# GpSimd's splits of the weights and of the heads' operands issued in two pieces

## The chip, the cores and the metric

The kernel runs on one core of one Trainium2 chip. The metric is the device time of one execution in microseconds, as the median of several executions. Only one core runs, so there is no traffic between cores.

## The reference

Two blocks follow each other on one sequence of 1024 tokens with 1024 features, in float32. The first has a mixer (attention with 8 heads in three dilated windows, beside a diagonal state-space branch) and a gated feed-forward part with a short convolution. The second has three gated branches and a final norm. Cut to what the change touches:

```python
def _hybrid_mixer(u, w_in, ...):
    proj = u @ w_in                       # q, k, v, us and two gates
    q, k, v, us, g_att, g_ssm = jnp.split(proj, ...)
    o_att = <windowed attention of q, k, v, 8 heads of 64>
    y_att = o_att @ w_proj_att
    y_ssm = _s5_branch(us, ...) @ w_proj_ssm
    merged = sigmoid(g_att + gb_att) * y_att + sigmoid(g_ssm + gb_ssm) * y_ssm
    return merged @ w_out
# h = x + gt1 * _hybrid_mixer(...);  h = h + gt2 * _conv_ffn(_modulate(h, ...))
# then the second block: p = h @ w_in_2, three branches, merged @ w_o, norm
```

## The kernel before

Every large product is made from two halves of each operand: a high part (the value rounded to the type `fp32r` that TensorE reads fast) and a low part (the value less its high part). A product is three matmuls: high by high, high by low and low by high. The activations' parts lie in `act_h` and `act_l`, the weights' in `w_h` and `w_l`. Weights come in units of 256 output columns: SyncE loads one unit into `raw`, GpSimd (POOL in the profile) makes `w_h` and `w_l` of it, and TensorE (PE) uses it. `w_h` and `w_l` have two buffers, so the split of unit n waits until PE has finished unit n-2, and PE's unit n waits for the split of unit n.

Units are numbered through the program: unit 0 is the state-space input, 1 to 6 are q, k and v (`N_QKV`), 7 to 14 the gates (`N_GATE`), 15 to 18 the projections (`N_PROJ`, six rows of 128 instead of eight), 19 to 22 the mixer's output (`N_OUT`), 23 and 24 the first two of the feed-forward part (`N_FFN`). After these, weights are split in another way (`unit_weights` and `block_lows`, 512 columns in one instruction), up to the last four units (`N_WO`).

`split` handles a unit in two parts. Each part is a TENSOR_SCALAR that writes `w_h` (multiply by 1.0, which rounds), a wait on its own semaphore, and a TENSOR_TENSOR that writes `w_l`. The first part raises `w_half`, the second `w_split`. A part of a unit with eight rows of 128 is 4 x 256 = 1024 columns, of a projection unit 3 x 256 = 768, and of a unit with four rows 512. PE waits for `w_split` in `split_done` before it loads the unit's first weights.

In attention GpSimd also runs `stage(h)` for each head: five dependent instructions over 1024 columns on `q2`, `k_ll` and `k_hh`. PE needs head h staged before that head's first scores. Meanwhile PE fills the gaps between score, transpose and value matmuls with the gate units' matmuls, and VectorE (DVE) works through the first block's modulation weights in `ada_chunks`: a chain of 128x256 instructions that read two operands in SBUF (`ada_part` and a chunk of `w_ada`). Behind them on DVE's queue stand the copies of transposed probabilities (`near_half`, L2864), which PE waits for in `values`.

The mixer's output units 19 and 20 are used for all tokens, but units 21 and 22 for half the tokens at a time. So PE comes to unit 22 after four half products of 24 matmuls, the first of which starts when unit 20 is done:

```python
for th in range(2):
    for u in range(4):
        if th == 0:
            split_done(N_OUT + 2 + u // 2)
            pe.wait_ge(s["out_read"], AHEAD + u + 1)
        ...
        product_half(slot(u), 1 - u // 2, u % 2, KD, act_h, act_l, th, after=after)
```

The orders of all engines are written out by hand; nothing is scheduled by a planner. `single(n)` is `split` with the wait for PE's unit n-2 (`units_before(n - 1)`). DVE's residual sums and sums of squares (L2992, L3002) run beside the output units.

Of the kernel before, what the change touches and what calls it, by code (L numbers as in the profile page):

```python
# [8 lines left out]
ALU = mybir.AluOpType  # L9
F32 = mybir.dt.float32  # L10
# [3 lines left out]
T = 1024  # L14
D = 1024
KD = D // P
HALF = 512
# [73 lines left out]
def splits_before(n):  # L91

    return n - blocks_before(n) - min(max(n - N_DB, 0), DB)
# [78 lines left out]
def build(nc, a, out):  # L172
    ctx = ExitStack()
    with ctx:
# [3 lines left out]
        def at(name, shape, offset, dt=F32):  # L178

            return nc.alloc_sbuf_tensor_at(name, shape, dt, offset=base + offset)  # L180
# [6 lines left out]
        w_h = at("w_h", [P, 2, KD, NB], 64 * kib, F32R)  # L187
        w_l = at("w_l", [P, 2, KD, NB], 80 * kib, F32R)
# [89 lines left out]
        q2 = at("q2", [P, 2, T], 96 * kib, F32R)  # L278
        k_hh = at("k_hh", [P, 2, T], 104 * kib, F32R)
# [109 lines left out]
        s = {n: ctx.enter_context(nc.semaphore(n)) for n in names}  # L389
# [52 lines left out]
        def raw_of(n):  # L442

            return raw[:, 0 if N_GATE + 1 < n < N_PROJ + 2 else n % 2]
# [586 lines left out]
        def _(pool):  # L1031
# [9 lines left out]
            def split(n, k, landed, before=None, kc=KD, landed_ssm=None):  # L1041

                src = raw_of(n)
                pool.wait_ge(w_in_[k], landed)
                if landed_ssm:
                    pool.wait_ge(ws_in[k], landed_ssm)
                if before is not None:
                    pool.wait_ge(s["gemm"], before)
                pool.sem_inc(s["passed"], 1)
                for half, done in enumerate((s["w_half"], s["w_split"])):  # L1050
                    c = slice(half * kc // 2, (half + 1) * kc // 2)
                    nc.gpsimd.tensor_scalar(w_h[:, k, c, :], src[:, c, :], 1.0, None, ALU.mult).then_inc(s["w_high"], 1)  # L1052
                    pool.wait_ge(s["w_high"], 2 * splits_before(n) + half + 1)
                    nc.gpsimd.tensor_tensor(w_l[:, k, c, :], src[:, c, :],  # L1054
                                            w_h[:, k, c, :].bitcast(F32), ALU.subtract).then_inc(done, 1)

            def split_first():

# [46 lines left out]
            def single(n, kc=KD, landed_ssm=None):  # L1105
                split(n, n % 2, 16 * (n // 2 + 1), units_before(n - 1) if n >= 2 else None, kc, landed_ssm)

            stage_step = Steps(pool, s["staged"])
            stage_step.base = PREP_STEPS

            def stage(h):

                e = h % 2
                own, other = slice(0, HD), slice(HD, P)
                pool.wait_ge(head_in[e], 4 * 16 * (h // 2 + 1))
                q, k = q2[:, e, :], k_ll[:, e, :]
                stage_step(nc.gpsimd.tensor_scalar(k_hh[:, e, :], q.bitcast(F32), 1.0, None, ALU.mult))
                stage_step(nc.gpsimd.tensor_tensor(q2[other, e, :], q2[other, e, :].bitcast(F32),
                                                   k_hh[other, e, :].bitcast(F32), ALU.subtract))
                stage_step(nc.gpsimd.tensor_scalar(q2[own, e, :], q2[own, e, :].bitcast(F32), 1.0, None, ALU.mult))  # L1120
                stage_step(nc.gpsimd.tensor_scalar(k_hh[:, e, :], k.bitcast(F32), 1.0, None, ALU.mult))
                stage_step(nc.gpsimd.tensor_tensor(k, k.bitcast(F32), k_hh[:, e, :].bitcast(F32), ALU.subtract))

            pool.wait_ge(s["consts_ready"], CONSTS)
            pool.wait_ge(s["g_row_in"], 16)
# [7 lines left out]
            for n in range(1, N_GATE - 1):  # L1133
                single(n)
            stage(0)
            single(N_GATE - 1)
            stage(1)
            single(N_GATE)
            single(N_GATE + 1)
            for h in range(2, HEADS):  # L1140
                stage(h)
                single(N_GATE + h)
# [33 lines left out]
            def single_behind(n, m, i, kc):  # L1176

                pool.wait_ge(s["prod_done"], NPRE * (i - 1) + (5 if m else 2))
                split(n, n % 2, 16 * (n // 2 + 1), None, kc)
# [2409 lines left out]
```

## Time and profile before

| | |
|---|---|
| median of 3 executions | 1994.09 us (1992.82 to 1998.42) |
| profiled execution, its own time | 1995.31 us |
| span in its profile | 1993.6 us |
| granted TensorE clock | 0.999 |
| PE busy | 1971.0 us, 99% |
| DVE busy | 1143.7 us, 57% |
| ACT busy | 668.1 us, 34% |
| POOL busy | 1319.6 us, 66%, 795 instructions |

The profiled execution's own time is 1.7 us above its span, and 1.2 us above the median. Engines work side by side, so the busy times don't add up. PE's share says that TensorE is nearly always at work; another engine counts only where PE waits for it. In the timelines a row gives start, duration, engine, line, operation, output and inputs and, in brackets, how long the engine was idle before and what ended that. PEld is PE's loading of weights, which runs one matmul ahead.

### The profile page before, as it was taken

How to read it: one execution, taken by the hardware profiler on the slowest of the kernel's cores; microseconds unless marked ns; L12 is line 12 of the kernel's file. 1: busy time of each engine (PE TensorE's matmuls, PEld its weight loads, DVE VectorE, ACT ScalarE, POOL GpSimd, SP SyncE). 2: the span in 40 equal slices, each digit the busy share in tenths (PEclk: the TensorE clock that was granted, in tenths of full speed). 3: DMA queues.
4: the chain of work that ended last, by engine and by line, in shares of the span. 5: the costliest groups of instructions: out<-in, count | busy, mean ns of one | idle time of the engine just before them, and what ended most of it. 6: DMA issues, size and time to landing. Idle time of an engine off the chain costs nothing. (4 is left out here: it accounts for less than half of the span.)

```text
span 1993.6 us, 26010 instructions
## 1 busy us (share of the span) xinstructions
PE 1971.0 (99%) x10105; PEld 1639.9 (82%) x10105; DVE 1143.7 (57%) x1363; ACT 668.1 (34%) x1115; POOL 1319.6 (66%) x795
## 2 busy tenths in 40 slices
PE   8999999999999999999999999999999999999998
PEld 6888888888888787888888898888788888888888
DVE  6962378767652676656575386722464554624554
ACT  5213233233421454444321145433434433211103
POOL 4647457655364459999746538877787888858650
PEclk9999999999999999999999999999999999999999
DMA  9645564563644213333664422333323323198332
GB/s 336 201 118 160 172 185 151 159 199 115 216 161 156 85 64 106 103 130 106 234 251 159 148 86 64 119 115 112 120 77 136 127 85 106 34 377 317 117 137 86
DMA packets 195979, 295.41 MB, mean 148 GB/s; under 512 B 15416, under 2 KB 147472, under 8 KB 195856
## 3 DMA queue, kind: packets, MB, share of 16 engines
q1 hardware_dynamic: 185488, 270.55, 40.4%
q10 hardware_dynamic: 10368, 23.19, 3.1%
q8 instruction: 81, 1.33, 0.3%
q14 instruction: 42, 0.34, 0.1%
HBM read 213.73 MB, written 79.97 MB: 147 GB/s over the span
## 5 line engine op out<-in xcount | busy, mean ns | idle before, releaser
L1668 PE MATMUL ps<-tb,w_h 128*128 128x512 f32 x1344 | 416.9, 391 | 2.5 <-DVE quads L3056 1.9
L1052 POOL TENSOR_SCALAR w_h<-raw 128x512 fp32r<-128x512 f32 (+2 forms) x100 | 225.5, 2255 | 282.8 <-issue 127.1
L1173 POOL TENSOR_TENSOR w_l<-raw,w_h 128x512 fp32r<-128x512 f32 x210 | 309.5, 1483 | 92.6 <-ACT w_h L2307 92.6
L1668 PEld LDWEIGHTS ps<-tb,w_h 128*128 128x128 f32 x1344 | 251.3, 188 | 59.2 <-issue 3.9
L1668 PE MATMUL ps<-tb,w_l 128*128 128x512 f32 x672 | 261.5, 389 | 0.0
L2307 ACT ACTIVATE w_h<-raw 128x512 fp32r<-128x512 f32 x210 | 130.8, 627 | 236.8 <-PE ps L1668 150.3
L1668 PE MATMUL ps<-act_h,w_h 128*128 128x512 f32 x504 | 196.3, 389 | 0.6 <-ACT quads L2336 0.5
L1054 POOL TENSOR_TENSOR w_l<-raw,w_h 128x512 fp32r<-128x512 f32 (+2 forms) x100 | 191.3, 1913 | 8.3
L1668 PE MATMUL ps<-act_l,w_h 128*128 128x512 f32 x504 | 196.1, 389 | 0.0
L1668 PE MATMUL ps<-act_h,w_l 128*128 128x512 f32 x504 | 196.1, 389 | 0.0
L1668 PEld LDWEIGHTS ps<-tb,w_l 128*128 128x128 f32 x672 | 126.1, 188 | 26.3
L1241 PE MATMUL ps<-act_h,w_h 128*128 128x512 f32 x352 | 139.1, 395 | 0.8 <-DVE act_l L2671 0.5
L1241 PE MATMUL ps<-act_l,w_h 128*128 128x512 f32 x352 | 137.1, 389 | 0.0
L1241 PE MATMUL ps<-act_h,w_l 128*128 128x512 f32 x352 | 137.1, 389 | 0.0
L1668 PEld LDWEIGHTS ps<-act_h,w_h 128*128 128x128 f32 x504 | 94.6, 188 | 21.2 <-ACT quads L2336 1.1
L1668 PEld LDWEIGHTS ps<-act_h,w_l 128*128 128x128 f32 x504 | 94.6, 188 | 19.6
L1668 PEld LDWEIGHTS ps<-act_l,w_h 128*128 128x128 f32 x504 | 94.6, 188 | 19.5
L1340 PE MATMUL ps<-act_h,w_h 128*128 128x512 f32 x256 | 102.0, 398 | 1.3
L1340 PE MATMUL ps<-act_h,w_l 128*128 128x512 f32 x256 | 100.2, 391 | 0.0
L1340 PE MATMUL ps<-act_l,w_h 128*128 128x512 f32 x256 | 100.2, 391 | 0.0
L3056 DVE TENSOR_TENSOR quads<-ps,quads 128x512 f32<-128x512 f32 x42 | 28.9, 688 | 118.4 <-ACT quads L2333 116.5
L1173 POOL TENSOR_TENSOR w_l<-sum,w_h 128x512 fp32r<-128x512 f32 x56 | 79.4, 1419 | 20.1 <-ACT w_h L2307 18.0
(455 smaller groups left out, 4581.2 us busy)
## 6 DMA issues: line engine op xcount, KB each, us to landing
raw<-in_w_in SPq DMA_DIRECT2D x44, 1024.0 KB, 5.3
raw<-in_w_up SPq DMA_DIRECT2D x16, 1024.0 KB, 5.2
f_scratch<-r SPq DMA_DIRECT2D x16, 1024.0 KB, 8.3
gates_scratch<-quads SPq DMA_DIRECT2D x24, 512.0 KB, 7.6
r<-gates_scratch SPq DMA_DIRECT2D x12, 1024.0 KB, 6.4
ada_lo<-in_w_ada SPq DMA_DIRECT2D x16, 512.0 KB, 4.1
ada_hi<-in_w_ada SPq DMA_DIRECT2D x16, 512.0 KB, 4.4
gates_scratch<-gate_st ACTq DMA_DIRECT2D x32, 256.0 KB, 3.0
```

The source lines that it names most:

```text
L1052: nc.gpsimd.tensor_scalar(w_h[:, k, c, :], src[:, c, :], 1.0, None, ALU.mult).then_inc(s["w_high"], 1)
L1054: nc.gpsimd.tensor_tensor(w_l[:, k, c, :], src[:, c, :], w_h[:, k, c, :].bitcast(F32), ALU.subtract).then_inc(done, 1)
L1173: nc.gpsimd.tensor_tensor(w7_l[:, SLOTS[o]], x, w7_h[:, SLOTS[o]].bitcast(F32), ALU.subtract)\
L1241: last = nc.tensor.matmul(dst[:, tok], w[:, k, kw + c, P * cg:P * cg + P], x[:, c, tok], start=(c == 0 and p == 0), stop=(c == kc - 1 and ...
L1340: last = nc.tensor.matmul(gate_bank(g), w[:, n % 2, c, P * (j % 2):P * (j % 2) + P], x[:, c, tok], start=(c == 0 and p == 0), stop=(c == K ...
L1668: last = nc.tensor.matmul(bank_of(n, bank), w[:, SLOTS[o], c, :], x(c), start=(first and c == 0 and p == 0), stop=(c == KD // 2 - 1 and p ...
L2307: A.activation(w7_h[:, SLOTS[o]], src, ACT.Copy).then_inc(s["w7_high"], 1)
L3056: v.tensor_tensor(quad(n, 1), bank_of(n, "b"), quad(n, 0), ALU.add).then_inc(s["q_done"], 1)
```

## The change

Each of `split`'s two instructions for a part is issued as pieces of at most 512 columns, and each of `stage`'s five over 1024 columns as two over 512. Semaphores are raised only by the last piece, so every wait stands where it stood. A part of 1024 columns becomes two pieces of 512, one of 768 becomes 512 and 256, and one of 512 stays whole. `split_first`, `split_half`, `unit_weights` and `block_lows` are not touched. The other engines' instructions are the same.

```diff
@@ -1049,10 +1049,14 @@
                 pool.sem_inc(s["passed"], 1)
                 for half, done in enumerate((s["w_half"], s["w_split"])):
                     c = slice(half * kc // 2, (half + 1) * kc // 2)
-                    nc.gpsimd.tensor_scalar(w_h[:, k, c, :], src[:, c, :], 1.0, None, ALU.mult).then_inc(s["w_high"], 1)
+                    pairs = [slice(i, min(i + 2, c.stop)) for i in range(c.start, c.stop, 2)]
+                    for i in pairs:
+                        last = nc.gpsimd.tensor_scalar(w_h[:, k, i, :], src[:, i, :], 1.0, None, ALU.mult)
+                    last.then_inc(s["w_high"], 1)
                     pool.wait_ge(s["w_high"], 2 * splits_before(n) + half + 1)
-                    nc.gpsimd.tensor_tensor(w_l[:, k, c, :], src[:, c, :],
-                                            w_h[:, k, c, :].bitcast(F32), ALU.subtract).then_inc(done, 1)
+                    for i in pairs:
+                        last = nc.gpsimd.tensor_tensor(w_l[:, k, i, :], src[:, i, :], w_h[:, k, i, :].bitcast(F32), ALU.subtract)
+                    last.then_inc(done, 1)
 
             def split_first():
 
@@ -1112,14 +1116,25 @@
 
                 e = h % 2
                 own, other = slice(0, HD), slice(HD, P)
+                halves = (slice(0, HALF), slice(HALF, T))
                 pool.wait_ge(head_in[e], 4 * 16 * (h // 2 + 1))
                 q, k = q2[:, e, :], k_ll[:, e, :]
-                stage_step(nc.gpsimd.tensor_scalar(k_hh[:, e, :], q.bitcast(F32), 1.0, None, ALU.mult))
-                stage_step(nc.gpsimd.tensor_tensor(q2[other, e, :], q2[other, e, :].bitcast(F32),
-                                                   k_hh[other, e, :].bitcast(F32), ALU.subtract))
...
-                stage_step(nc.gpsimd.tensor_tensor(k, k.bitcast(F32), k_hh[:, e, :].bitcast(F32), ALU.subtract))
+                for tok in halves:
+                    last = nc.gpsimd.tensor_scalar(k_hh[:, e, tok], q[:, tok].bitcast(F32), 1.0, None, ALU.mult)
+                stage_step(last)
+                for tok in halves:
+                    last = nc.gpsimd.tensor_tensor(q2[other, e, tok], q2[other, e, tok].bitcast(F32),
+                                                   k_hh[other, e, tok].bitcast(F32), ALU.subtract)
+                stage_step(last)
...
+                for tok in halves:
+                    last = nc.gpsimd.tensor_tensor(k[:, tok], k[:, tok].bitcast(F32), k_hh[:, e, tok].bitcast(F32), ALU.subtract)
+                stage_step(last)
```

On GpSimd, at the split of unit 22 and the start of the split of unit 23, these instructions stood before (the brackets name the semaphores that an instruction waits for; `gemm` counts PE's finished products, `w_in` the landed loads):

```order
L1052 TENSOR_SCALAR w_h<-raw 128x1024 [waits w_in0,gemm]
L1054 TENSOR_TENSOR w_l<-raw,w_h 128x1024 [waits w_high]
L1052 TENSOR_SCALAR w_h<-raw 128x1024
L1054 TENSOR_TENSOR w_l<-raw,w_h 128x1024 [waits w_high]
L1052 TENSOR_SCALAR w_h<-raw 128x1024 [waits w_in1,gemm]
```

and these stand there now:

```order
L1054 TENSOR_SCALAR w_h<-raw 128x512 [waits w_in0,gemm]
L1054 TENSOR_SCALAR w_h<-raw 128x512
L1058 TENSOR_TENSOR w_l<-raw,w_h 128x512 [waits w_high]
L1058 TENSOR_TENSOR w_l<-raw,w_h 128x512
L1054 TENSOR_SCALAR w_h<-raw 128x512 x2
L1058 TENSOR_TENSOR w_l<-raw,w_h 128x512 [waits w_high]
L1058 TENSOR_TENSOR w_l<-raw,w_h 128x512
L1054 TENSOR_SCALAR w_h<-raw 128x512 [waits w_in1,gemm]
```

Each part's one instruction has become two. The second piece waits for nothing, and the wait on `w_high` stands ahead of the first subtracting piece as it stood ahead of the whole one.

On GpSimd, at the staging of a head in attention and the split of a gate unit behind it, these stood before:

```order
L1117 TENSOR_SCALAR k_hh<-q_128 128x1024
L1118 TENSOR_TENSOR q_128<-q_128,k_hh 64x1024
L1120 TENSOR_SCALAR q_128<-q_128 64x1024
L1121 TENSOR_SCALAR k_hh<-k_ll 128x1024
L1122 TENSOR_TENSOR k_ll<-k_ll,k_hh 128x1024
L1052 TENSOR_SCALAR w_h<-raw 128x1024
L1054 TENSOR_TENSOR w_l<-raw,w_h 128x1024
L1052 TENSOR_SCALAR w_h<-raw 128x1024
L1054 TENSOR_TENSOR w_l<-raw,w_h 128x1024
```

and these stand there now:

```order
L1123 TENSOR_SCALAR k_hh<-q_128 128x512 x2
L1126 TENSOR_TENSOR q_128<-q_128,k_hh 64x512 x2
L1130 TENSOR_SCALAR q_128<-q_128 64x512 x2
L1133 TENSOR_SCALAR k_hh<-k_ll 128x512 x2
L1136 TENSOR_TENSOR k_ll<-k_ll,k_hh 128x512 x2
L1054 TENSOR_SCALAR w_h<-raw 128x512 x2
L1058 TENSOR_TENSOR w_l<-raw,w_h 128x512 x2
L1054 TENSOR_SCALAR w_h<-raw 128x512 x2
L1058 TENSOR_TENSOR w_l<-raw,w_h 128x512 x2
```

The order is the same, each row is now two instructions of half the columns, and a head's ten pieces and the gate unit's eight run one after the other.

## Rows read from the trace of the kernel before

**Rows 1.** Busy us and instructions of each engine, clock, DMA: two stretches.
```profile
220.00:550.00 330.00, 325.37 (x2026) 272.48 (x2025) 229.90 (x384) 113.04 (x237) 180.90 (x71) 1.00 0.53 163
550.00:680.00 130.00, 130.00 (x579) 107.07 (x579) 61.36 (x63) 32.63 (x41) 72.16 (x28) 1.00 0.40 145
```

**Rows 2.** Groups of POOL instructions by shape: busy us, mean ns, idle before.
```profile
L1052 POOL TENSOR_SCALAR w_h<-raw 128x1024 fp32r<-128x1024 f32 x44 | 129.4, 2941 | 145.4 <-issue 75.9 <-DMA raw<-in_w_o 21.5 <-DMA raw<-in_w_in 16.5
L1054 POOL TENSOR_TENSOR w_l<-raw,w_h 128x1024 fp32r<-128x1024 f32 x44 | 109.1, 2480 | 3.7
```

**Rows 3.** Timeline of POOL: 512-column instructions, undisturbed.
```profile
682.96 1.29 POOL L1164 TENSOR_TENSOR sum_f<-sum_f,raw 128x512 f32<-128x512 f32 x1
684.20 1.30 POOL L1165 TENSOR_TENSOR raw<-raw 128x512 f32<-128x512 f32 x1
...
1769.56 1.50 POOL L1052 TENSOR_SCALAR w_h<-raw 128x512 fp32r<-128x512 f32 x1 [10.60 <-PE ps L1949]
1771.14 1.29 POOL L1054 TENSOR_TENSOR w_l<-raw,w_h 128x512 fp32r<-128x512 f32 x1
```

**Rows 4.** Timeline of POOL at the split of unit 22.
```profile
625.65 2.78 POOL L1052 TENSOR_SCALAR w_h<-raw 128x1024 fp32r<-128x1024 f32 x1 [9.50 <-issue]
628.52 2.40 POOL L1054 TENSOR_TENSOR w_l<-raw,w_h 128x1024 fp32r<-128x1024 f32 x1
630.89 2.77 POOL L1052 TENSOR_SCALAR w_h<-raw 128x1024 fp32r<-128x1024 f32 x1
633.74 2.40 POOL L1054 TENSOR_TENSOR w_l<-raw,w_h 128x1024 fp32r<-128x1024 f32 x1
```

**Rows 5.** Timeline of PE's weight loads: the first of unit 22.
```profile
636.19 0.19 PEld L1241 LDWEIGHTS ps<-act_h,w_h 128*128 128x128 f32 x1 [0.27 <-POOL w_l L1054]
```

**Rows 6.** Timeline of DVE in the same stretch: the sums of squares.
```profile
626.77 1.22 DVE L3002 TENSOR_TENSOR acc<-acc,sq 128x1024 f32<-128x1024 f32 x1
...
631.68 1.32 DVE L3002 TENSOR_TENSOR acc<-acc,sq 128x1024 f32<-128x1024 f32 x1
```

**Rows 7.** The split of unit 23: POOL's last instruction, PE's first load.
```profile
668.39 2.41 POOL L1054 TENSOR_TENSOR w_l<-raw,w_h 128x1024 fp32r<-128x1024 f32 x1
...
670.85 0.19 PEld L1241 LDWEIGHTS ps<-act_h,w_h 128*128 128x128 f32 x1 [0.29 <-POOL w_l L1054]
```

**Rows 8.** The split of unit 7: POOL's last instruction, PE's first load.
```profile
216.58 2.38 POOL L1054 TENSOR_TENSOR w_l<-raw,w_h 128x1024 fp32r<-128x1024 f32 x1
...
219.06 0.19 PEld L1340 LDWEIGHTS ps<-act_h,w_h 128*128 128x128 f32 x1
```

**Rows 9.** POOL and DVE at the split of unit 19.
```profile
571.64 3.75 POOL L1052 TENSOR_SCALAR w_h<-raw 128x1024 fp32r<-128x1024 f32 x1
...
570.65 2.10 DVE L2978 TENSOR_TENSOR act_l<-mix,act_h 128x1024 f32 x1 [1.25 <-ACT act_h L2254]
```

**Rows 10.** Splits with a small lead (units 1 and 99): POOL's end, PE's first load.
```profile
57.64 2.39 POOL L1054 TENSOR_TENSOR w_l<-raw,w_h 128x1024 fp32r<-128x1024 f32 x1
...
61.48 0.19 PEld L1241 LDWEIGHTS ps<-act_h,w_h 128*128 128x128 f32 x1
...
1932.09 2.39 POOL L1054 TENSOR_TENSOR w_l<-raw,w_h 128x1024 fp32r<-128x1024 f32 x1
...
1935.80 0.19 PEld L1241 LDWEIGHTS ps<-act_h,w_h 128*128 128x128 f32 x1
```

**Rows 11.** A wait in attention: POOL, DVE and PE.
```profile
345.63 2.96 POOL L1122 TENSOR_TENSOR k_ll<-k_ll,k_hh 128x1024 fp32r<-128x1024 f32 x1
...
346.72 3.40 DVE L2912 SCALAR_TENSOR_TENSOR ada_part<-ada_hi,c_act,ada_part 128x256 f32<-128x256 f32 x2
...
350.85 0.49 PE L1445 MATMUL ps<-ones,ada_part 128*128 128x1 f32 x3 [0.97 <-DVE prob_t L2864]
```

**Rows 12.** The modulation's accumulations by tile, 300 to 313 us: duration min/median/max in ns.
```profile
L2912 DVE SCALAR_TENSOR_TENSOR ada_part<-ada_hi,c_act,ada_part x4: 485/1180/2042, 304.8 to 310.9; 128x256 f32<-128x256 f32 x4
```

**Rows 13.** Who PE waited for in attention, 220 to 550 us: us, times, longest.
```profile
PE ps L1445 <- DVE prob_t L2864: 2.5, 5, 1.0
```

More of the change, by code:

```diff
@@ L1114, in stage @@
                 own, other = slice(0, HD), slice(HD, P)
+                halves = (slice(0, HALF), slice(HALF, T))
                 pool.wait_ge(head_in[e], 4 * 16 * (h // 2 + 1))
                 q, k = q2[:, e, :], k_ll[:, e, :]
-                stage_step(nc.gpsimd.tensor_scalar(k_hh[:, e, :], q.bitcast(F32), 1.0, None, ALU.mult))
-                stage_step(nc.gpsimd.tensor_tensor(q2[other, e, :], q2[other, e, :].bitcast(F32),
-                                                   k_hh[other, e, :].bitcast(F32), ALU.subtract))
-                stage_step(nc.gpsimd.tensor_scalar(q2[own, e, :], q2[own, e, :].bitcast(F32), 1.0, None, ALU.mult))
-                stage_step(nc.gpsimd.tensor_scalar(k_hh[:, e, :], k.bitcast(F32), 1.0, None, ALU.mult))
-                stage_step(nc.gpsimd.tensor_tensor(k, k.bitcast(F32), k_hh[:, e, :].bitcast(F32), ALU.subtract))
+                for tok in halves:
[6 more added lines that the diff above has]
+                for tok in halves:
+                    last = nc.gpsimd.tensor_scalar(q2[own, e, tok], q2[own, e, tok].bitcast(F32), 1.0, None, ALU.mult)
+                stage_step(last)
+                for tok in halves:
+                    last = nc.gpsimd.tensor_scalar(k_hh[:, e, tok], k[:, tok].bitcast(F32), 1.0, None, ALU.mult)
+                stage_step(last)
+                for tok in halves:
+                    last = nc.gpsimd.tensor_tensor(k[:, tok], k[:, tok].bitcast(F32), k_hh[:, e, tok].bitcast(F32), ALU.subtract)
+                stage_step(last)
             pool.wait_ge(s["consts_ready"], CONSTS)
```

## Prediction

> **What bounds the kernel now.** I read the page's busy times first: PE is busy for 99% of the span at a granted clock of 0.999, the upper of its two levels (2.4 GHz), so time can be won or lost only where PE stands still. The table by stretches says how much that is where the changed instructions run: in attention PE lacks 330.00 - 325.37 = 4.6 us, and in the projections and the mixer's output nothing [rows 1]. POOL is busy for 55% of both stretches (180.90 of 330, 72.16 of 130). Its load is no bound there; what counts is how long before PE's first weight load of a unit POOL's last piece of that unit ends. So I went through the timelines of POOL and of PE's weight loads, unit by unit, and kept the leads that are small, and then asked for what PE waited in attention.
>
> The leads: unit 22's last instruction ends at 633.74 + 2.40 = 636.14, and PE loads that unit's first weights at 636.19, having waited 0.27 us for this POOL instruction [rows 4, 5]. Unit 23's ends at 668.39 + 2.41 = 670.80, and PE loads at 670.85, again after a wait for it, 0.29 us [rows 7]. Unit 7's ends at 216.58 + 2.38 = 218.96, PE loads at 219.06, without a wait shown [rows 8]. Unit 1 has 1.45 us of lead (60.03 to 61.48) and unit 99 has 1.32 us (1934.48 to 1935.80) [rows 10]. Of the other changed units none has less than 1.8 us in the same two timelines, and most have 4 to 10 us; each head in attention is staged about 8 us before its first scores.
>
> Units 22 and 23 have no lead for a reason that the code shows. The split of unit 22 starts when PE has finished unit 20, and PE comes to unit 22 after 48 more matmuls. At 130 / 579 = 0.225 us each [rows 1] these are 10.8 us; the split takes 636.14 - 625.65 = 10.5 us and starts a little after PE's end. So PE waits for whatever is added to this split. Unit 23 is split when PE is done with unit 21, again with 48 matmuls and a few small ones between.
>
> **What the change costs on POOL.** It adds an instruction for each of 44 + 44 parts of 1024 columns [rows 2], 8 + 8 of 768, and 5 x 8 of staging: 144 in all. A piece of 512 columns costs more than half of 1024. Subtracting: 1.29 us against 2.40, and a piece with no wait behind it is followed by the next after 684.20 - 682.96 = 1.24 us [rows 3, 4]. So two pieces take 1.24 + 1.29 = 2.53, 0.13 more. Rounding: 1.50 us against 2.77; with the same overlap of 0.05 that is 1.45 + 1.50 = 2.95, 0.18 more. A whole split of eight rows gets 2 x (0.13 + 0.18) = 0.6 us longer, and a head's staging 3 x 0.18 + 2 x 0.13 = 0.8 us. No row shows two rounding pieces back to back. If their fixed parts overlapped fully the price would be 0; if each piece paid the whole 0.23 us by which two times 1.50 exceed 2.77, and the 0.09 us between dependent instructions (628.52 less 628.43) as well, it would be 0.32. I take 0.18, since it has the subtracting rows' form.
>
> Total for POOL is about 144 x 0.16 = 23 us, of which all but the units named above lie under PE's work: a gate unit with its head's staging ends 1.4 us later and has 8.
>
> **What of it PE sees.** Unit 7: 0.6 us less the lead of 0.1, so 0.5. No DVE instruction with two SBUF operands runs in that split. Unit 23: 0.6, all of it; DVE there reads one operand in PSUM, and POOL's durations are undisturbed. Unit 22: 0.6, and something else. Two sums of squares on DVE (`acc` and `sq`, both in SBUF) run in this split, at 626.77 and 631.68 [rows 6]. Today they start 1.1 and 0.8 us into a rounding instruction of POOL and disturb nothing: 1.22 us is their plain time, and the second takes 0.1 more. So a rounding instruction of 1024 columns stands in DVE's way only for its first 0.9 us. With pieces, the second starts at 625.65 + 1.45 = 627.10, into the middle of the first sum (until 627.99), and the second part's first piece starts at 630.89 + 0.3 + 0.8 = 632.0, into the second sum (until 632.9). What such a meeting costs POOL is 3.75 - 2.77 = 0.98 us at unit 19, where a waiting DVE instruction entered between two POOL instructions that stood back to back [rows 9]. Two meetings of 0.9 and 0.9 us overlap give 0.75 and 0.85. So unit 22 loses 0.6 + 1.6 = 2.2 us; its bounds are 0.6 (no meeting) and 0.6 + 2 x 0.98 = 2.6. I take 2.0.
>
> **The Trainium skill** on the same place, "SBUF — State Buffer", section "Who interferes with whom": VectorE with two SBUF inputs and a GpSimd instruction that reads SBUF exclude each other, and the second to come is blocked until the first has finished. By that the sum at 626.77 would have ended at 628.43 + 1.2 = 629.6; the row has it ending at 627.99, so for the rounding form the trace disagrees, and for the subtracting form, below, it agrees. By the page's rule the sums would be the ones to wait, unit 22 would lose 0.6 us only, and my total would be 1.6 us lower.
>
> Unit 1 has 1.45 us for 0.6 us of pieces and whatever DVE puts between them; I count 0.1. Unit 99 has 1.32 us for 0.6: nothing. Losses: 0.5 + 2.0 + 0.6 + 0.1 = 3.2 us.
>
> **What it gives back.** In attention PE waited five times, 2.5 us in all, for DVE's copy of transposed probabilities [rows 13]. One of them: POOL subtracts from 345.63 to 348.59; DVE's two accumulations start at 346.72 and take 3.40 us together, where each takes 0.485 undisturbed; the copy stands behind them, and PE waits 0.97 us [rows 11, 12]. A subtracting instruction does hold DVE to its end. With pieces the first accumulation is let in at the boundary, at about 346.3 + 1.3 = 347.6, and ends at 347.9; the second piece then has the port until 349.2, and the second accumulation ends at 349.5 in place of 350.1. That is 0.6 us of 0.97; over the five, capped by each wait, up to 2. But POOL also comes 0.5 us later in each head and may meet other accumulations, and two heads without such a wait can get one. Bounds: 2.5 us gained, 0.5 lost; I take 1.1 gained, a little above the middle, since the one meeting that is worked out gains.
>
> **Sum.** 3.2 - 1.1 = 2.1 us. On the profiled execution: span 1993.6 + 2.1 = 1995.7, own time 1995.31 + 2.1 = 1997.4. That execution is 1.2 us above the median of 1994.09, so the forecast for the median is 1996.2 us, 0.1% more. What a measurement of this kernel can tell from no change is about 0.3%, 6 us: its three runs spread over 5.6.
>
> **Rivals.**
>
> Slower by over 6 us: the pieces' price. All hangs on what one added instruction costs in units 7, 22 and 23, which have twelve of them (four each). At a price x PE loses 12x plus unit 22's meetings of 1.6, and beyond 0.36 also 4x - 1.45 at unit 1 and beyond 0.33 4x - 1.32 at unit 99, less 0.1 of lead and 1.1 given back: 20x - 2.4 in all, which is 6 us at x = 0.42. At 0.5 it is 7.6 us: 2001.7. For it speaks that no row has two rounding pieces in a row; against it that 0.32 us is the most that these rows give.
>
> Not slower at all, because DVE gains as much as PE loses: unit 22 has no meetings (0.6), losses are 1.8, and attention gives 2.0. That is 1993.9. For it speaks that DVE's sums follow PE, and a small shift of POOL misses them; against it that the first meeting needs only the piece's start to be later by 0 to 0.9 us than 626.77, and it is later by 0.3. The rule of the Trainium skill named above would bring this rival about.
>
> Faster by over 6 us: PE's waits in attention are 4.6 us at most, and those elsewhere do not hang on POOL. I see no mechanism, only the spread of measurements.
>
> The change does nothing on the chip, because pieces run as one: POOL's busy time would stay at 1320. It has 0.02; the time would be 1994.
>
> **How the numbers follow.** Forecast of a small loss, 1994.5 to 1999: 0.64. Cancelled or slightly gained, 1992 to 1994.5: 0.24. Slower rival: 0.08. Nothing on the chip: 0.02. Faster by over 6 us: 0.02. Range for 8 in 10: the sum's lower bound is 0.4 + 0.6 + 0.6 - 2.5 = -0.9 and its upper 0.5 + 2.6 + 0.6 + 0.8 + 0.5 = 5.0; with 1 us of spread of a median to either side, 1992.2 to 2000.1. The cases give faster by over 0.3% 0.02, within 0.3% 0.89, slower 0.09.
>
> **What would show it in the profile after.** POOL: 939 instructions, busy some 20 us longer; groups of 512-column pieces of `w_h` at about 1.5 us and `w_l` at 1.3. PE's first load of unit 22 about 2 us after its last load of unit 20's pass, with a wait for POOL named; of unit 23 about 0.6; the first gate unit with a wait of about 0.5. A rounding piece of over 2 us at the two sums of squares. DVE's accumulations shorter on average, with none near 2.5 us, and PE waiting less than 2.5 us for the copies. The prediction is wrong if unit 22's pieces run undisturbed, if other waits of PE for POOL appear in the projections, or if the price of a piece is far from 0.16 us.

## The result, and the profile after it

The changed kernel takes 2003.26 us (median of 10 runs, 1999.02 to 2008.74) against 1994.89 us for the kernel before. The ratio is 1.0042, with a 95% interval of 1.0031 to 1.0053: a loss of 8.4 us, 6.2 to 10.6. (One of the ten executions of the kernel before took 2181.17 us; the medians hardly feel it.) The forecast was 1996.2 us and the range ended at 2000.1, so the loss is four times the 2.1 us that I gave, outside the range, and on the side (slower by over 0.3%) that had a chance of 0.09.

The page of the changed kernel: span; busy us, share and instructions of each engine.

```profile
span 2001.4 us, 26154 instructions
PE 1972.0 (99%) x10105; PEld 1641.5 (82%) x10105; DVE 1114.7 (56%) x1363; ACT 668.7 (33%) x1115; POOL 1347.5 (67%) x939
```

POOL has the 939 instructions that were forecast and is busy for 1347.5 us, 27.9 more than before, where the prediction had 23. DVE is busy for less than before (1143.7 then): from 220 to 520 us its accumulations on `ada_lo` (L2912, now L2927) take 593 ns on average instead of 996. The prices of a piece came out as worked out (two rounding pieces take 2.95 us, two subtracting ones 2.5, in the rows of a head below). The groups of POOL by shape (busy us, mean ns | idle before), which answer to [rows 2]:

```profile
L1054 POOL TENSOR_SCALAR w_h<-raw 128x512 fp32r<-128x512 f32 x144 | 226.4, 1583 | 264.0 <-issue 124.2 <-PE ps L1256 22.3 <-DMA raw<-in_w_o 21.7
L1058 POOL TENSOR_TENSOR w_l<-raw,w_h 128x512 fp32r<-128x512 f32 x144 | 199.6, 1399 | 8.3
```

The stretches of [rows 1] (busy us and instructions of PE, PEld, DVE, ACT, POOL; clock, DMA share, GB/s):

```profile
220.00:550.00 330.00, 322.83 (x2020) 271.64 (x2021) 203.44 (x385) 113.44 (x237) 199.40 (x142) 1.00 0.53 163
550.00:680.00 130.00, 127.38 (x563) 104.53 (x562) 61.38 (x62) 33.56 (x40) 73.30 (x50) 1.00 0.36 128
```

In the attention stretch PE now lacks 330.00 - 322.83 = 7.2 us where it lacked 4.6. In the second stretch it lacks 2.6 where it lacked nothing.

The split of unit 22 and PE's first load of that unit, which answer to [rows 4, 5]:

```profile
629.31 3.69 POOL L1054 TENSOR_SCALAR w_h<-raw 128x512 fp32r<-128x512 f32 x2 [8.69 <-issue]
633.08 2.54 POOL L1058 TENSOR_TENSOR w_l<-raw,w_h 128x512 fp32r<-128x512 f32 x2
635.58 3.92 POOL L1054 TENSOR_SCALAR w_h<-raw 128x512 fp32r<-128x512 f32 x2
639.59 2.49 POOL L1058 TENSOR_TENSOR w_l<-raw,w_h 128x512 fp32r<-128x512 f32 x2
...
642.13 0.19 PEld L1256 LDWEIGHTS ps<-act_h,w_h 128*128 128x128 f32 x1 [2.56 <-POOL w_l L1058]
```

DVE's sums of squares in it, which answer to [rows 6]:

```profile
630.43 1.22 DVE L3017 TENSOR_TENSOR acc<-acc,sq 128x1024 f32<-128x1024 f32 x1
...
635.34 1.36 DVE L3017 TENSOR_TENSOR acc<-acc,sq 128x1024 f32<-128x1024 f32 x1
```

The two pairs of rounding pieces take 3.7 and 3.9 us instead of 2.95: these are the two meetings with the sums of squares that the prediction worked out, and PE's wait for POOL goes from 0.27 to 2.56 us. To see how PE's delay grows, I set the start of each of the 10105 matmuls after against the same matmul before. The difference grows by 2.3 us at unit 22 and by 0.6 at unit 23 (forecast: 2.0 and 0.6), and by 0.3 at unit 7 (forecast: 0.5). (PE's idle time there, which the views of waits give, is a little less: 2.1 and 0.5 us.)

What the forecast did not have lies in attention. Who PE waited for there:

```profile
PE ps L1569 <- DVE prob_t L2879: 4.2, 3, 2.2
PE ps L1355 <- POOL w_l L1058: 1.5, 2, 1.3
...
PE ps L1460 <- DVE prob_t L2879: 0.4, 1, 0.4
```

The wait of [rows 13] is nearly gone (L1460 is L1445 of before, 0.4 us for 2.5). Two others have come: for DVE's copies of other tiles, and for POOL's split of gate units, which had a lead of 8 us before. So the question is where that lead went. One head of the kernel before, in order: the last instruction of a gate unit's split, SyncE's issues of the next gate load and of the next head's operands, the start of that head's staging, the first and last instruction of the next split, and PE's first load of that unit.

```profile
318.84 2.40 POOL L1054 TENSOR_TENSOR w_l<-raw,w_h 128x1024 fp32r<-128x1024 f32 x1
...
321.34 0.37 SPq L625 DMA_DIRECT2D raw<-in_w_in  x1
323.92 0.37 SPq L703 DMA_DIRECT2D ada_lo<-in_w_ada  x1
324.38 0.47 SPq L692 DMA_DIRECT2D q<-qk_scratch  x1
...
334.48 2.78 POOL L1117 TENSOR_SCALAR k_hh<-q 128x1024 fp32r<-128x1024 f32 x1 [13.24 <-DMA k_ll<-qk_scratch]
...
348.81 2.77 POOL L1052 TENSOR_SCALAR w_h<-raw 128x1024 fp32r<-128x1024 f32 x1 [0.22 <-POOL k_ll L1122]
...
356.85 2.39 POOL L1054 TENSOR_TENSOR w_l<-raw,w_h 128x1024 fp32r<-128x1024 f32 x1
...
366.91 0.19 PEld L1340 LDWEIGHTS ps<-act_h,w_h 128*128 128x128 f32 x1 [0.30 <-issue]
```

The same head of the changed kernel (its previous split ended at 326.50):

```profile
326.60 0.37 SPq L625 DMA_DIRECT2D raw<-in_w_in  x1
327.02 0.72 SPq L703 DMA_DIRECT2D ada_lo<-in_w_ada  x1
327.83 0.48 SPq L692 DMA_DIRECT2D q<-qk_scratch  x1
...
339.96 2.95 POOL L1123 TENSOR_SCALAR k_hh<-q 128x512 fp32r<-128x512 f32 x2 [13.46 <-DMA k_ll<-qk_scratch]
...
355.66 2.95 POOL L1054 TENSOR_SCALAR w_h<-raw 128x512 fp32r<-128x512 f32 x2 [0.22 <-POOL k_ll L1136]
...
364.24 3.10 POOL L1058 TENSOR_TENSOR w_l<-raw,w_h 128x512 fp32r<-128x512 f32 x2
...
367.39 0.19 PEld L1355 LDWEIGHTS ps<-act_h,w_h 128*128 128x128 f32 x1 [0.40 <-POOL w_l L1058]
```

This is a closed loop. SyncE's queue holds the next gate unit's weight load until `w_split` is raised, and behind it in the same queue stand the next head's four operand loads. They have to land before the staging, and behind the staging stands the next split. Before, the head loads left 3.1 us after the split's end (324.38 less 321.24). Their own wait for PE's scores was over by then; they stood behind the load of `ada_lo`, and that one waited for DVE's accumulations. SyncE's only wait from 321.4 to 324.5 us:

```profile
SPq L703 <- DVE ada_part L2912: 2.2, 1, 2.2
```

The landing took 10.1 us, the staging 14.3, the split 10.4. With the 1.33 us that SyncE takes where nothing holds it (below), the loop can run in 1.33 + 10.10 + 14.33 + 10.43 = 36.2 us, and PE needs 36.7 to 38 us a head: PE sets the pace, and the lead of 366.91 less 359.24 = 7.7 us is made anew in each head. After, the head loads leave 1.33 us behind the split, with the gate load's megabyte just ahead of them, and land in 12.13; the staging takes 15.70 and the split 11.68. That is 40.8 us, longer than PE's head. The lead shrinks in each head, and at 367.34 the split ends 0.05 us before PE loads.

One head is one sample. Over the six heads whose staging starts from 249 to 446 us, landing, staging and split take 9.4, 14.0 and 10.7 us on average before and 10.6, 15.0 and 11.8 after; with the same 1.33 the loop is 35.5 us before and 38.7 after. PE's head, 36.7 us where nothing holds it up, lies between the two in every reading.

What SyncE waited for from 220 to 520 us, before and after (us in total, times, longest):

```profile
SPq L624 <- POOL w_l L1054: 21.9, 5, 5.0
```

```profile
SPq L624 <- POOL w_l L1058: 54.1, 5, 13.2
```

A late loop costs twice. Once the lead is gone PE waits for the split. And SyncE, standing at the gate load, is late for all that is behind it, too: the loads of `ada_lo` and `ada_hi` then leave in one burst with the gate's and the head's. In the changed kernel:

```profile
371.68 0.43 SPq L703 DMA_DIRECT2D ada_hi<-in_w_ada  x1
...
383.94 1.11 DVE L2927 SCALAR_TENSOR_TENSOR ada_part<-ada_hi,c_act,ada_part 128x256 f32<-128x256 f32 x1 [4.68 <-DMA ada_hi<-in_w_ada]
...
386.67 0.52 PE L1569 MATMUL ps<-ident,prob 128*128 128x128 f32 x3 [2.23 <-DVE prob_t L2879]
```

`ada_hi` lands 12 us after its issue, DVE stands idle for it for 4.68 us with the copy of `prob_t` behind the accumulation, and PE waits 2.23 us for the copy. The other two of these waits, 0.99 us at 424.25 and 0.96 at 462.44, follow the same way: DVE stood idle 2.12 and 2.91 us for `ada_hi`, and its two accumulations then took 3.03 and 2.25 us beside POOL's staging pieces, where two undisturbed ones take 1.0.

In the projections, on the other hand, the pieces gain something that the forecast did not have. PE's waits at L1241 for DVE's `mod` and `o_l`, 0.4 and 0.5 us, are gone. DVE's pair of `o_l` before, while POOL splits unit 16 in whole instructions, and the same pair in the changed kernel (one takes 1.22 us undisturbed):

```profile
519.75 4.00 DVE L2933 TENSOR_TENSOR o_l<-o_raw,o_h 128x1024 fp32r<-128x1024 f32 x2
```

```profile
524.13 2.86 DVE L2948 TENSOR_TENSOR o_l<-o_raw,o_h 128x1024 fp32r<-128x1024 f32 x2
```

The two waits stand in all ten traces with whole projection splits (before and runs 1 and 4 to 11) and in none of the three with pieces there (the changed kernel, runs 2 and 3). PE gains 1.1 to 1.2 us by it from 510 to 525 us in each of the three.

### The profile page after: what moved, and what is told of

It is laid out like the page before. It is cut to its first block and busy times, and to the rows that moved or that the text cites. A ratio compares the mean times of both kernels' runs of the same rounds, so it can differ in the third digit from the quotient of the medians.

```text
span 2001.4 us, 26154 instructions
## 1 busy us (share of the span) xinstructions
PE 1972.0 (99%) x10105; PEld 1641.5 (82%) x10105; DVE 1114.7 (56%) x1363; ACT 668.7 (33%) x1115; POOL 1347.5 (67%) x939
## 3 DMA queue, kind: packets, MB, share of 16 engines
q8 instruction: 81, 1.33, 0.3%
## 5 line engine op out<-in xcount | busy, mean ns | idle before, releaser
L1054 POOL TENSOR_SCALAR w_h<-raw 128x512 fp32r<-128x512 f32 (+1 forms) x152 | 233.4, 1547 | 264.0 <-issue 124.2
L1058 POOL TENSOR_TENSOR w_l<-raw,w_h 128x512 fp32r<-128x512 f32 (+1 forms) x152 | 207.3, 1379 | 8.3
L1683 PEld LDWEIGHTS ps<-tb,w_l 128*128 128x128 f32 x672 | 126.2, 188 | 26.5
L1188 POOL TENSOR_TENSOR w_l<-sum,w_h 128x512 fp32r<-128x512 f32 x56 | 79.5, 1420 | 20.1 <-ACT w_h L2322 18.0
```

Of the source, the lines that this page charges most:

```text
L1054: last = nc.gpsimd.tensor_scalar(w_h[:, k, i, :], src[:, i, :], 1.0, None, ALU.mult)
L1058: last = nc.gpsimd.tensor_tensor(w_l[:, k, i, :], src[:, i, :], w_h[:, k, i, :].bitcast(F32), ALU.subtract)
L1188: nc.gpsimd.tensor_tensor(w7_l[:, SLOTS[o]], x, w7_h[:, SLOTS[o]].bitcast(F32), ALU.subtract)\
L1683: last = nc.tensor.matmul(bank_of(n, bank), w[:, SLOTS[o], c, :], x(c), start=(first and c == 0 and p == 0), stop=(c == KD // 2 - 1 and p ...
```

## The experiments

Ratios are to runs of the kernel before on the same chip. **Theory L** is the loop. **Theory P** says that only the price of the pieces counts, where POOL was late already (units 7, 22, 23). **Theory S** came from the traces: at 40 us, before any changed instruction, the changed kernel's PE is 3.2 us behind (the expectations have 3.3).

**1. Pieces only in the heads** (staging, and the splits of units 7 to 14).

```
-  pairs = [slice(i, min(i + 2, c.stop)) for i in range(c.start, c.stop, 2)]
+  pairs = [slice(i, min(i + 2, c.stop)) for i in range(c.start, c.stop, 2)] if N_GATE <= n < N_PROJ else [c]
```

> Pieces in the staging of all eight heads and in the splits of gate units 7 to 14 only; every other split whole. Theory L (the loop): from one w_split through the gate load, the head loads behind it in SyncE's queue, their landing, the staging and the next split the loop took 36.2 us before, shorter than TensorE's 36.7 to 38.0 us a head; with pieces it takes 40.8 us, so the lead of some 8 us is eaten head by head and then TensorE waits. It expects 3.5 to 5.5 us more than before, ratio 1.0018 to 1.0028, and w_split's lead over TensorE's need under 1 us from unit 11 on. Theory P (the price only where GpSimd was late already: units 22 and 23): at most 1 us more, ratio 1.0000 to 1.0005. Theory S (the 3.3 us lost in the first 40 us, before any changed instruction, belong to the longer program and come with every build of it): about 1.0015 more on top of either.

Measured: 2001.53 us, ratio 1.0031 (1.0020 to 1.0041). Three quarters of the loss are here, a little more than L gave (1.0028 at most), and P with its 1.0005 is out. The lead fell to 0.6 us at unit 12, not yet at 11 (the table behind run 8).

**2. The complement.**

```
-  halves = (slice(0, HALF), slice(HALF, T))
+  halves = (slice(0, T),)
...
+  pairs = [...] if not N_GATE <= n < N_PROJ else [c]
```

> The complement: staging and gate units whole, pieces in the splits of units 1 to 6, 15 to 24 and the later whole-width splits. Theory L: 2.1 us at unit 22 and 0.7 at unit 23, some 3 us more than before, ratio 1.0012 to 1.0018, and nothing in the heads. Theory P: all of the change's loss, 7 to 9 us, ratio 1.0035 to 1.0045. Theory S: 3 us more at the start, ratio near 1.003.

Measured: 1996.94 us, ratio 1.0008 (0.9999 to 1.0017). Waits of PE from 550 to 700 us in its trace, the 2.1 of unit 22 and the rest of unit 23:

```profile
PE ps L1256 <- POOL w_l L1058: 2.6, 2, 2.1
```

P, which had the whole loss here, is out a second time. L had 1.0012 to 1.0018, so the median lies below its range. What L left out is the gain in the projections: PE loses 2.3 + 0.6 us at units 22 and 23 and gains 1.1 before them, 1.8 us in sum, and 1.0008 is 1.6 us. 1.0031 and 1.0008 add to 1.0039, the whole change has 1.0042: two places, and they add. Theory S would have put 3 us into both kernels. None of the other traces with pieces has them: PE is 0.2 us behind at 60 us in runs 1 and 2 (0.7 at 40 us in run 2), and 0.5 ahead in run 3, with every piece in it. They belonged to that one execution.

**3. The changed kernel with the head loads ahead of the gate load** in SyncE's queue. `head(h)` and `head_bias(h)` with their waits are issued at `t % NH == 4`, before `load_gate(m)`, and no longer at `t % NH == 5`.

```
+  h = t // NH + 2
+  if t % NH == 4 and h < HEADS:
+      sp.wait_ge(s["s_ready"], NH * (h - 1))
+      sp.wait_ge(s["sm_ready"], AHEAD + NH * (h - 1))
+      head(h)
+      head_bias(h)
   m = t // NH + 2
   if t % NH == 4:
       ... load_gate(m) or proj(m - KD), as before
...
-  h = t // NH + 2
-  if t % NH == 5 and h < HEADS:
-      ...
```

> The changed kernel with one thing moved: in SyncE's queue the loads of a head's operands stand ahead of the next gate unit's weight load instead of behind it, so that they wait for the scores alone and not for w_split too. Theory L: the loop is cut, w_split's intervals fall back to TensorE's 37 to 38 us and the leads stay above 4 us; the loss in the heads goes, the let-ins' gain stays, so 0 to 3 us above before, ratio 1.0000 to 1.0018. Theory P: no change against the changed kernel, ratio 1.0042. A third way: the gate weights now land later, behind the head loads on the DMA engines, and the split waits for them instead; then w_split is as late as it was and the ratio is 1.003 to 1.005.

Measured: 1994.77 us, ratio 1.0007 (0.9995 to 1.0018). All pieces are in it, POOL's pieces cost what they did (1587 and 1420 ns on average in the splits, against 1583 and 1399), and with one move in a queue most of the loss is gone. SyncE's wait for POOL at the gate load, 54.1 us in the changed kernel, is not in its trace, nor is any wait of PE for POOL in attention. This is the run that shows the loop. What it does not show by itself is how much of its 7 us comes from cutting the loop and how much from the other place in the head at which staging and split now fall; the next run shows that the place has an effect of its own.

**4. The kernel before with the same move.**

> The kernel before with the same move of the head loads. Theory L: TensorE set the pace there already (leads of 7.6 to 8.3 us), so nothing is won: ratio 0.9993 to 1.0005, with the lead of w_split grown by some 4 us. Theory P: the same. If the late gate weights cost something, 1.001 to 1.002.

Measured: 2004.05 us (five executions), ratio 1.0039 (1.0025 to 1.0052). Neither theory had this. The leads grew to 17.6 us, so it is not the loop. PE's head took 39 us in four of the five heads of the table behind run 8, and what PE waited for from 220 to 550 us was DVE's copies:

```profile
PE ps L1554 <- DVE prob_t L2864: 5.9, 5, 1.4
PE ps L1445 <- DVE prob_t L2864: 5.0, 5, 1.1
```

One of these waits, on POOL, DVE and PE:

```profile
306.99 2.44 POOL L1054 TENSOR_TENSOR w_l<-raw,w_h 128x1024 fp32r<-128x1024 f32 x1
...
307.21 3.68 DVE L2912 SCALAR_TENSOR_TENSOR ada_part<-ada_hi,c_act,ada_part 128x256 f32<-128x256 f32 x2
310.92 0.69 DVE L2864 COPY prob_t<-ps 128x512 f32<-128x512 f32 x1
...
311.76 0.52 PE L1554 MATMUL ps<-ident,prob 128*128 128x128 f32 x3 [1.40 <-DVE prob_t L2864]
```

POOL subtracts, DVE's two accumulations (0.5 us each undisturbed) take 3.68 us together, the copy is behind them, PE is behind the copy. It is a meeting of the kind in [rows 11], and it comes twice in each of five heads. Staging and split now begin at another place of PE's head; runs 9 to 11 ask whether that is why.

**5. Heads only, and the head loads first** (edits 1 and 3 together).

> Pieces in the staging and in the gate units 7 to 14 alone, and the head loads ahead of the gate load: the third run without the 2.1 us at unit 22 and the 0.7 at unit 23 that the second and third run's traces show. Theory L2 (the loop through SyncE's queue makes the change slow; and where in a head the staging falls decides how often it stands before a VectorE copy that TensorE waits for, which pieces cure): TensorE keeps 36.7 us a head as in the third run, against 37.4 on average before, so 2 to 4.5 us less than before, ratio 0.9978 to 0.9993. Theory P (only the price counts): 1.0000 to 1.0010.

Measured: 1994.24 us against 1996.81, ratio 0.9987 (0.9978 to 0.9996): 2.6 us faster than the kernel before, the best ratio of the study, in the range of L2 and outside that of P. In its trace the gate load follows the head loads at once (the last of them is issued at 320.36, the gate load at 321.07).

**6. Pieces in the staging alone**, queue as before (`pairs = [c]` in every split): half of the price.

> Pieces in the staging alone, every split whole, queue order as before. Half of the price: the loop is 36.2 us and some 0.7 to 2.3 (landing included), 36.9 to 38.5, against TensorE's 36.7 when it isn't held up. Theory L2: w_split's lead falls by 0.2 to 1.8 us a head from about 8 and stays above 0 for all or most heads, while the let-ins take TensorE's waits; ratio 0.9990 to 1.0012, far from the 1.0031 of all pieces in the heads. Theory D (what harms is the pieces' own meetings with VectorE in the staging): most of the loss is still here, 1.002 to 1.003.

Measured: 1995.27 us, ratio 0.9997 (0.9987 to 1.0008), in L2's range and below theory D's 1.002. The lead falls from 7.8 to 0.5 us and is used up just as attention ends.

**7. The price without the pieces.** The kernel before, with one more instruction for each head (and `STAGED`, the number of staging steps, 6 instead of 5).

```
+  stage_step(nc.gpsimd.tensor_scalar(k_hh[:, e, 0:HALF], q[:, 0:HALF].bitcast(F32), 1.0, None, ALU.mult))
   stage_step(nc.gpsimd.tensor_scalar(k_hh[:, e, :], q.bitcast(F32), 1.0, None, ALU.mult))
```

> No piece anywhere: the kernel before with the first 512 columns of the first rounding done twice in each head's staging (one more GpSimd instruction of 1.5 us a head, which is about the price of the nine extra pieces of a head; the result is the same). Theory L2: the loop is 36.2 and 1.6, with a later landing up to 39.5 us, against TensorE's 37.4 us a head of before; the leads fall by 0.5 to 2 us a head and the staging moves later in the head: 1 to 6 us more than before, ratio 1.0005 to 1.0030. Theory D: the time was in the pieces' own meetings, not in their price: 0.9998 to 1.0005.

Measured: 1999.05 us, ratio 1.0011 (1.0001 to 1.0021). Its trace at the last gate unit:

```profile
451.16 1.49 POOL L1117 TENSOR_SCALAR k_hh<-q 128x512 fp32r<-128x512 f32 x1 [12.00 <-DMA k_ll<-qk_scratch]
...
477.83 0.19 PEld L1341 LDWEIGHTS ps<-act_h,w_h 128*128 128x128 f32 x1 [0.53 <-POOL w_l L1054]
```

No piece, and yet the last gate unit has no lead left and PE waits for POOL: 1.5 us a head are enough to eat it. SyncE's wait at the gate load is 44.7 us here, against 21.9 before. The ratio's interval only just leaves 1.0000, so the lead is the stronger evidence. Its interval also touches theory D's range, so it is the leads here and the ratio of run 6 that put D (the pieces' own meetings with DVE) out as the main cause. The loss is smaller than in run 1, and so is what was added to the loop: staging and split together take 26.5 us a head on average here, 26.9 in run 1 and 24.8 before.

**8. The kernel before, once more**, for a second trace.

> The kernel before, unchanged, for a second trace. Both theories: ratio 1.0000 within 0.0010. If the place of the staging in the head (stage start 42 to 43 us after TensorE's first use of the unit before) and the 37.4 us a head are the kernel's own, they come again; if they hang on how the transfers landed, they come out between the 40.5 us and 36.7 us a head that the second run's trace had with the same instructions in the heads.

Measured: 1994.97 us, ratio 0.9993 (0.9983 to 1.0002), span 1993.1. Who PE waited for in attention:

```profile
PE ps L1445 <- DVE prob_t L2864: 0.5, 2, 0.3
```

The 2.5 us of [rows 13], from which my gain was worked out, are 0.5 us here, with no line changed.

The leads of gate units 9 to 14, each PE's first load less the end of the unit's split, in us, and PE's mean head (first loads of units 9 and 14, a fifth of the difference), taken from the timelines of all these traces:

```
run                                   lead at unit 9    10    11    12    13    14   PE's head
kernel before                                    7.7   7.7   7.7   8.2   8.2   8.4   37.4
8  kernel before, again                          8.4   8.2   8.2   8.4   8.2   8.4   37.0
2  pieces outside the heads                      8.7   8.4   8.2   8.3   8.2   8.4   37.0
changed kernel                                   7.2   4.1   0.0   0.6   0.6   0.0   37.9
1  pieces in the heads                           6.5   5.4   3.0   0.6   0.0   0.0   37.8
6  pieces in the staging                         7.8   7.3   5.1   3.8   1.2   0.5   36.8
7  price without pieces                          7.7   5.3   2.8   2.4   1.2   0.0   37.2
3  changed, head loads first                    13.4  12.9  13.4  13.3  13.3  12.9   36.7
5  pieces in the heads, head loads first        13.3  13.3  13.3  13.3  13.3  12.1   36.7
4  before, head loads first                     17.6  17.6  17.6  17.6  17.6  13.5   38.5
```

With the old order of the queue and nothing added to the heads the lead stays, with anything added it runs down, and with the new order it stays at 12 us or more, in runs 9 to 11 too.

**9 and 10. What the fourth run lost.** Both have the head loads first; 9 has pieces in the staging alone, 10 in the gate units' splits alone.

> The head loads ahead of the gate load, pieces in the staging alone, the splits whole. It asks why the fourth run (whole instructions, head loads first) lost 0.4%. Theory W (whole splits): in its trace the whole 1024-column subtraction of a gate unit's split at 307.0 us holds the second of three accumulations of VectorE, and the copy behind them, for which TensorE waits 1.4 us; the splits are whole here too, so most of it stays: ratio 1.0015 to 1.0035. Theory V (whole staging): it was the staging's instructions; cured here, 0.9980 to 1.0000.

> The head loads ahead of the gate load, the staging whole, pieces in the splits of gate units 7 to 14 alone. Theory W: the subtraction lets VectorE in after 512 columns, so TensorE's head takes 37 us or less again: ratio 0.9985 to 1.0005. Theory V: still 1.0025 to 1.0040.

Measured: 1992.68 us, ratio 0.9992 (0.9983 to 1.0001), and 1993.85 us, 0.9993 (0.9984 to 1.0002). Either half takes the loss away, so W and V both fall: it was no one instruction.

**11. Whole instructions, head loads first, and the extra instruction of run 7.**

> Whole instructions with the head loads ahead of the gate load (the fourth run, which lost 0.4%), and the first 512 columns of each staging's first rounding done twice (1.6 us more of GpSimd a head, the result is the same). Since pieces in the staging alone and in the splits alone each took that loss away, two causes are left. Theory F (where it falls): the whole instructions stood before VectorE's copies only by the place at which they fell; 1.6 us later in the head they miss them, and the ratio is 0.9985 to 1.0010. Theory I (it is the let-ins): any piece in the head breaks up the queue of VectorE and GpSimd, a later start does not; the ratio stays 1.0025 to 1.0050.

Measured: 1995.66 us, ratio 1.0003 (0.9993 to 1.0013), head 37.0 us. This is the fourth run with more work on POOL, and it is 7 us faster (1.0039 less 1.0003). So it was the place in the head at which the whole instructions fell, theory F, and not the want of let-ins. With the head loads first, PE's scores and DVE's row maxima of them (`neg_max`) release them, so POOL's instructions fall at the same place of every head, and a bad place repeats: head 2's staging starts at 250.9 us in run 4 and at 250.6 in run 11, but what stands behind its first instruction comes 1.6 us later in run 11. Whether the pieces of runs 9 and 10 helped by letting DVE in, or likewise by being some 0.6 us longer, stays open.

## Why the prediction was wrong

**The step that failed** is the sentence on the total for POOL: "a gate unit with its head's staging ends 1.4 us later and has 8". I took the 8 us as a store from which each head draws anew. It is one store for all heads: it is refilled only while the loop through SyncE's queue is shorter than PE's head. In the head shown it had 0.5 to 1.8 us to spare. There the landing came 2.0 us later and staging and split took 2.6 us longer: 1.4 by the price of the pieces, 1.2 more while DVE's instructions stood among them. On average of six heads these are 1.2 and 2.0 us, against some 1.2 us to spare (36.7 less 35.5). I had read the leads from POOL's and PE's timelines and never followed what starts the staging: the page names the k_ll transfer as its releaser, and that transfer stands in a queue behind a wait for POOL itself. The signs that I gave for being wrong looked for new waits for POOL in the projections; they came in attention.

What it costs: in the heads (222 to 480 us) the changed kernel's PE falls behind by 1.9 us against the profiled execution of before, and by 4.4 us against the second one (run 8), which had hardly a wait in attention to begin with. The projections give 1.1 us of it back. The third run, with the loop cut, is 7 us below the changed kernel by the ratios (1.0042 less 1.0007).

**The price of a piece** was right: two rounding pieces 2.95 us, two subtracting 2.54. The rival built on a higher price did not happen, though the time came out on its side.

**Unit 22** was right in kind and size: forecast 2.0, worked out 2.2, measured 2.3. The meetings happened at both sums, and POOL was the one lengthened (3.69 and 3.92 us for 2.95), while the first sum, which began 1.1 us after POOL's first piece, ran in its plain 1.22 us. The Trainium skill, "SBUF — State Buffer", section "Who interferes with whom", has the later of the two wait for the earlier's end: the trace agrees for POOL's second piece and for the piece that began 0.24 us into the second sum, and disagrees for the sum that began inside the first piece. **Unit 23**: 0.6 for 0.6. **Unit 7**: 0.3 for 0.5; but the same step is 0.6 in run 8, with nothing changed, and 1.7 in run 1, so a trace can't size it to a few tenths.

**The gain of 1.1 us** had no firm ground. The wait for these copies did fall, from 2.5 to 0.4 us. But run 8 has 0.5 with whole instructions and run 2 has 0.5 with whole instructions in the heads, so most of the 2.5 was the one execution's: in three heads its staging lay 42 to 43 us behind PE's first load of the unit two before, in theirs always at 41.5 or less. That PE did gain 1.1 us from DVE's side, in the projections, is luck: the prediction named no wait there. A wait that is there in one trace is no stock to gain from.

**The range** added bounds for each term and none for the lead. Against run 8 the profiled execution of the changed kernel is 8.3 us longer. Of these the heads give 4.4, units 22 and 23 give 2.9, and the projections take 1.1 off: 6.2. Another 2.6 us stand there at 60 us, before any changed instruction on which PE waited; the granted clock of that execution was 0.83 from 20 to 30 us, against 1.00 before. Runs 1 to 3 have no such loss, so I count it as the execution's; the interval on the 8.4 (6.2 to 10.6) does not contradict that, and does not prove it.

## What to carry to other kernels

A lead is slack against one delay, and a stock against a repeated one. Before a small cost is called hidden in a loop, follow what starts the hidden work back through the transfers and the queue in which they are issued; if it comes back to the same work, sum the loop and compare it with the consumer's period: what counts is the difference of the two (here 0.5 to 1.8 us a head), not the lead (8 us). In SyncE's queue, where each issue waits for the one ahead of it, an issue that waited for POOL stood ahead of the loads which POOL needed next; moving it helped only together with something else, since the move alone cost the kernel before 0.4% (run 4). And before a gain is claimed from waits that one trace shows, look whether a second execution has them.

## What the runs showed of the hardware

**When DVE and POOL meet, a few hundredths of a microsecond can decide which of them is held up.** At the end of the first pass of the feed-forward part, where no line differs, PE's wait for DVE is 1.1 us in some executions and 2.2 in others, of the same code. The kernel before (DVE, then POOL):

```profile
780.42 0.72 DVE L3073 TENSOR_TENSOR r<-quads 128x512 f32<-128x512 f32 x1 [9.38 <-DMA f_scratch<-r]
...
780.68 1.63 POOL L1170 TENSOR_TENSOR raw<-raw,sum_f 128x512 f32<-128x512 f32 x1
```

Run 4, with the same instructions:

```profile
788.32 1.79 DVE L3073 TENSOR_TENSOR r<-quads 128x512 f32<-128x512 f32 x1 [9.70 <-DMA f_scratch<-r]
...
788.27 1.29 POOL L1170 TENSOR_TENSOR raw<-raw,sum_f 128x512 f32<-128x512 f32 x1
```

Where DVE is 0.26 us ahead it runs in 0.72 us and POOL's instruction takes 1.63 instead of 1.29. Where POOL is 0.05 us ahead it runs in 1.29 and DVE takes 1.79. That delay goes on to PE: the waits of PE in run 4 from 780 to 860 us, and the clock of that stretch, before and in run 4.

```profile
PE ps L1668 <- DVE quads L3056: 2.7, 2, 2.2
780.00:860.00 80.00, 76.78 (x329) 62.48 (x328) 45.94 (x40) 35.44 (x56) 70.65 (x47) 0.98 0.36 122
```

```profile
780.00:860.00 80.00, 78.75 (x346) 64.41 (x345) 48.76 (x44) 36.66 (x54) 73.77 (x48) 1.00 0.32 106
```

After the wait of 2.2 us the mean granted clock of the stretch is 0.98, so part of it ran at the lower of the two levels; after the one of 1.1 us it is 1.00. In runs 1, 2 and 7 it is the same (2.2 us and 0.98), which puts some 3 us into their traces there. In the changed kernel and in runs 8 and 10 the 2.2 us came without a fall of the clock. Unit 22 shows it too: behind PE's wait of 2.1 us the granted clock is 0.91 from 620 to 640 us in run 2, where PE loses 1.6 us more, and 1.00 around the same wait in the changed kernel and in run 3. So such a wait can cost its own length again and more, but need not. These differences lie in traces, one execution each; the medians decide between kernels.
